# A hybrid encoder step: norms that write into the sum, second projections that turn their own rows, and a residual that is fetched back

## The reference, cut to what matters

```
p = x @ w_in                                   # layer 0: 2560 columns, layer 1: 2888
layer 0: window attention with sinks  |  RWKV-7 time mixing
layer 1: differential attention (C)   |  attention to selected keys (D), picked by an indexer
mix = concat(...) @ w_out
x = layer_norm(ALPHA * x + mix, g1, b1)
h = square(relu(x @ w_up)) @ w_down            # 4096 wide
x = layer_norm(ALPHA * x + h, g2, b2)
```

## Time and profile before

| | |
|---|---|
| timed runs | 4241.22, 4242.47, 4243.46 us; median 4242.47 |
| profiled execution | 4249.11 us, its span 4247.2 us |
| busy share of the span | PE 84%, PEld 76%, DVE 49%, ACT 21%, POOL 4% |
| mean granted TensorE clock | 0.892 of 2.4 GHz |
| DMA | 142.17 MB, mean 33 GB/s |

### The profile page before, as it was taken

How to read it: one execution, slowest core, us unless ns; L and a number is a source line. 1 busy time by engine, 2 the same in 40 slices (tenths; PEclk the granted TensorE clock), 3 DMA queues, 4 the chain that set the end, 5 groups by cost and what they waited for, 6 DMA issues and landing times. The chain is left out here.

```text
span 4247.2 us, 61115 instructions
## 1 busy us (share of the span) xinstructions
PE 3561.4 (84%) x26473; PEld 3233.1 (76%) x26492; DVE 2089.8 (49%) x2992; ACT 909.3 (21%) x1681; POOL 174.7 (4%) x75
## 2 busy tenths in 40 slices
PE   7978499767999999989967777777556889999997
PEld 7977289666999999979954444554434889999996
DVE  4315966556223232441136788998565542323235
ACT  1016311112101001120024444443223120101011
POOL 0010000003000000100020000000000120000001
PEclk9988599878999999989966788887677999999998
DMA  3110000110111111111120000001111111111111
GB/s 100 41 62 5 0 5 4 47 40 25 40 45 45 46 40 45 35 40 43 37 72 1 1 1 1 1 1 30 40 40 25 35 32 44 45 46 45 43 43 47
DMA packets 244534, 142.17 MB, mean 33 GB/s; under 512 B 36101, under 2 KB 237978, under 8 KB 243770
## 3 DMA queue, kind: packets, MB, share of 16 engines
q1 hardware_dynamic: 243320, 138.22, 11.2%
q10 hardware_dynamic: 962, 0.20, 0.0%
HBM read 123.14 MB, written 15.32 MB: 33 GB/s over the span
## 5 line engine op out<-in xcount | busy, mean ns | idle before, releaser
L238 PE MATMUL psum<-rounded,rounded 128*128 128x364 f32 x13536 | 2283.6, 331 | 96.0 <-DVE rounded L744 42.9
L238 PEld LDWEIGHTS psum<-rounded,rounded 128*128 128x128 f32 x13536 | 2273.8, 189 | 107.0 <-issue 81.6
L617 ACT ACTIVATE arena<-psum 128x1092 f32<-128x1092 f32 x64 | 69.3, 1083 | 1216.0 <-PE psum L238 1216.0
L222 DVE CAST rounded<-arena 128x1024 fp32r<-128x1024 f32 x188 | 134.1, 713 | 358.0 <-PE psum L238 343.6
L631 DVE CAST rounded<-arena 128x1092 fp32r<-128x1092 f32 x64 | 46.7, 729 | 535.2 <-ACT arena L620 535.2
L224 DVE TENSOR_TENSOR rounded<-arena,rounded 128x1024 fp32r<-128x1024 f32 x188 | 282.2, 1501 | 6.5
L1388 PE MATMUL psum<-arena 64*64 64x64 f32 x8160 | 256.8, 220 | 23.9 <-POOL arena L1572 12.5
L2063 PE MATMUL psum<-arena 128*128 128x128 f32 (+2 forms) x1424 | 240.1, 323 | 40.5 <-ACT arena L2127 39.5
L1388 PEld LDWEIGHTS psum<-arena 64*64 64x64 f32 x8160 | 246.2, 136 | 35.4 <-DVE arena L1525 18.4
L2063 PEld LDWEIGHTS psum<-arena 128*128 128x128 f32 (+1 forms) x1424 | 215.9, 231 | 66.8 <-issue 37.5
L2047 PE MATMUL psum<-arena 128*128 128x128 f32 (+1 forms) x712 | 142.0, 336 | 139.8 <-ACT arena L2118 139.5
(11 more groups left out here) (230 smaller groups left out, 2762.9 us busy)
## 6 DMA issues: line engine op xcount, KB each, us to landing
arena<-in_w_ff_up SPq DMA_DIRECT2D x128, 256.0 KB, 3.1
arena<-in_w_ff_down SPq DMA_DIRECT2D x128, 256.0 KB, 3.1
arena<-in_w_in_odd SPq DMA_DIRECT2D x46, 256.0 KB, 3.3
arena<-in_w_in_even SPq DMA_DIRECT2D x40, 256.0 KB, 3.4
x_kept<-arena SPq DMA_DIRECT2D x1, 4368.0 KB, 12.4
arena<-x_kept SPq DMA_DIRECT2D x1, 4368.0 KB, 13.1
arena<-in_x_prompt SPq DMA_DIRECT2D x1, 4096.0 KB, 18.4
arena<-in_cache_c_k SPq DMA_DIRECT2D x4, 1024.0 KB, 5.6
```

The costliest lines, as they stand in the source:

```text
L222: nc.vector.tensor_copy(rounded(m, high), low).then_inc(self.weights_high, 1)
L238: last = nc.tensor.matmul(m.ps[:, out:out + TB], rounded(m, w)[:, k, :], rounded(m, x(k))[:, b * TB:(b + 1) * TB], start=(k == 0 and n == ...
```

## The change

The change was described as "mixing inside first projections, norms straight to the sum, second projections with turned rows; residual back later". The diff holds the following.

- `Norm`: no copy of the mean (L716 goes); the centre steps read it from PSUM; five of them stand ahead of the variance, one behind it, two behind the early weight split. Gain and shift are written to a destination `norm.dest`: `m.acc` in the MLPs, `p[:, 8:16]` in the second projections, `m.x` in the last norm. The low part still goes to `m.x`.
- `mlp`: GpSimd's additions and the wait for them go.
- `project_odd` is written out, 23 tiles in a new order: indexer keys and weights (72 columns, one tile), c keys, d keys, c values, d values, then the queries. Tile u - 2 is turned on TensorE inside tile u, at its operand tiles k = 1, 4 and 7, into PSUM banks 3 and 7; VectorE moves the rows of tile u - 3 after the weight split of tile u; SyncE stores key rows from two staging buffers, and all values at the end. The indexer keys are copied to the other 64 partitions by a DMA. The normalised x is written to DRAM (`x_kept`) once all high parts are made. The lambda is made here.
- `turn_rows` goes. `odd_attention` fetches x back at the start of its second block; it has other room for its buffers, and `m.p` has 18 tiles, not 24.
- `Ring` counts its loads per slot (23 is no multiple of 4).

`project_even` is not in the diff.

```diff
 class Norm:
-        act.wait_ge(self.P.sem, self.P.done(0, "mean"))
-        nc.scalar.activation(blocks(self.mean), linear_out(m, 0), ACT.Copy).then_inc(*self.A.step("copy"))
...
-            nc.scalar.activation(m.x[:, k, :], m.x[:, k, :], ACT.Identity, scale=m.col(self.gain + k),
+            nc.scalar.activation(self.dest[:, k, :], m.x[:, k, :], ACT.Identity, scale=m.col(self.gain + k),
...
-                nc.scalar.activation(rounded(m, high[:, k, :]), m.x[:, k, :], ACT.Copy).then_inc(ring.x_high, 1)
+                nc.scalar.activation(rounded(m, high[:, k, :]), self.dest[:, k, :], ACT.Copy).then_inc(ring.x_high, 1)
...
-            tt(m.x[:, k, :], self.source[:, k, :], self.mean, ALU.subtract)\
+            tt(blocks(m.x[:, k, :]), blocks(self.source[:, k, :]), linear_out(m, 0), ALU.subtract)\
...
-            tt(rounded(m, m.x[:, k, :]), m.x[:, k, :], rounded(m, high[:, k, :]), ALU.subtract)\
+            tt(rounded(m, m.x[:, k, :]), self.dest[:, k, :], rounded(m, high[:, k, :]), ALU.subtract)\
...
-        for k in range(3):
+        for k in range(5):
             centre(k)
...
-        centre(3)
+        centre(5)
...
-        for k in range(4, 8):
+        for k in range(6, 8):
             centre(k)
 def mlp(m, layer, norm):
+    norm.dest = m.acc
...
-            for k in range(8):
-                pool.wait_ge(ring.x_split, ring.operands + k + 1)
-                nc.gpsimd.tensor_tensor(m.acc[:, k, :], rounded(m, m.x[:, k, :]), rounded(m, high[:, k, :]), ALU.add)\
-                    .then_inc(residual, 1)
...
-                    dve.wait_ge(residual, layer * 8 + u + 1)
+ODD_TILES = ([("idx", 2816, 17)] + [("ck", 512 + 128 * a, 4 + a) for a in range(4)] + [("dk", 2048, 16)]
+             + [("cv", 1024 + 128 * a, 8 + a) for a in range(4)] + [("dv", 2176, 12)]
+             + [("cq", 128 * a, a) for a in range(4)] + [("iq", 2304 + 128 * a, 12 + a) for a in range(4)]
+             + [("dq", 64 * a, 8 + a) for a in range(4)])
 def project_odd(m, norm):
+    norm.dest = p[:, 8:16, :]
+    groups = [(0, 4), (4, 8), (8, 9)]
+    staged = [p[:, 14 + i, 0:512].rearrange("p (t c) -> p t c", t=4) for i in range(2)]
...
+            for u in range(tiles):                                   # SyncE
+                ring.load(sp, 0, u, True, lambda slot: loads(u, slot))
+                if u == 3:
+                    sp.wait_ge(ring.x_high, ring.operands + 8)
+                    sp.dma_start(io["x_kept"], p[:, 8:16, :].rearrange("p k t -> p (k t)")).then_inc(kept, 16)
+                v = u - 6
+                if v in keys:
+                    store_rows(v)
+                if v == keys[0]:
+                    sp.wait_ge(turned, group_at(v, 2) + 1)
+                    sp.dma_start(p[64:128, 17, :], p[0:64, 17, :]).then_inc(doubled, 16)
+                if v == ODD_TURNED[-1]:
+                    sp.wait_ge(rows, group_at(v, 2) + 1)
+                    store_values("c_v", m.vn)
+                    store_values("d_v", m.vd)
...
+            def turn(u, g):                                          # TensorE
+                n = group_at(u, g)
+                if n >= 2:
+                    pe.wait_ge(rows, n - 1)
+                pe.wait_ge(ring.freed, ring.tiles + u + 1)
+                for t in range(a, z):
+                    last = nc.tensor.transpose(...)
+                last.then_inc(turned, 1)
...
+                def ready(k):
+                    if u == 0:
+                        pe.wait_ge(ring.x_split, ring.operands + k + 1)
+                    if u - 2 in ODD_TURNED and k in (1, 4, 7):
+                        turn(u - 2, k // 3)
...
+            def move(u, g):                                          # VectorE
+                dve.wait_ge(turned, n + 1)
...
+                    to = stores_before(u, g)
+                    if to >= 2:
+                        dve.wait_ge(stored[to % 2], 16 * (to // 2))
...
+            for u in range(1, tiles):
+                ring.split(dve, 0, 0, u, True)
+                if u == 2:
...
+                    dve.wait_ge(kept, 16)
+                if u - 3 in ODD_TURNED:
+                    for g in range(len(groups)):
+                        move(u - 3, g)
-def turn_rows(m):
...
 def odd_attention(m):
+            sp.dma_start(m.arena[:, m.x_at:m.x_at + 8 * T], io["x_kept"]).then_inc(x_back, 16)
...
+            sp.wait_ge(x_back, 16)
             sp.wait_ge(f.O[1].sem, f.O[1].rounds(last_c.round + 4))
```

More of the change, by code:

```diff
@@ L199, in begin @@
         self.ndma = ndma
-        self.next = (self.pieces + pieces, self.loads + pieces // SLOTS * ndma * 16,
+        self.next = (self.pieces + pieces,
+                     [n + len(range(s, pieces, SLOTS)) * ndma * 16 for s, n in enumerate(self.loads)],
                      self.operands + 8, self.tiles + tiles)
@@ L217, in split @@
         low, high = self.low[:, u % SLOTS], self.high[:, u % HIGHS]
-        dve.wait_ge(self.loaded[u % SLOTS], fills * 16 * self.ndma + (self.loads + (u // SLOTS + 1) * 16 * self.ndma))
+        dve.wait_ge(self.loaded[u % SLOTS], fills * 16 * self.ndma + (self.loads[u % SLOTS] + (u // SLOTS + 1) * 16 * self.ndma))
         if not first or u >= HIGHS:
@@ L553, in mlp @@
     ring = m.linears.begin(w + 32 * T, 2, 64, 0)
-    relu, added, squared, hidden_rounded, hidden_split, residual = m.mlp_sems
+    relu, added, squared, hidden_rounded, hidden_split = m.mlp_sems
     had = layer * FF // 128
@@ L692, in tensor @@
         for b in range(NB):
-            last = nc.tensor.matmul(m.ps[:, b * 512:b * 512 + TB], m.c("mean"), m.sum[:, b * TB:(b + 1) * TB],
+            last = nc.tensor.matmul(m.ps[:, b * 512:b * 512 + TB], m.c("mean"), self.totals[0][:, b * TB:(b + 1) * TB],
                                     start=True, stop=True)
         last.then_inc(*self.P.step("mean"))
-        for v, total in enumerate((m.sum, m.square_sum)):
+        for v, total in enumerate(self.totals):
             for t, (b, o) in enumerate(self.spots):
@@ L1971, in queries @@
         t.penal = kind == "D" and t.nk > TOPK
-        t.qtile = 0 if kind == "C" else 12
+        t.qtile = 0 if kind == "C" else 8
         t.load = t.sample and kind == "C"
@@ L2009, in scores @@
         dist = (distS if t.sample else distP)[:, first:first + t.nk]
-        keys = kt_s if t.sample else flat(p[:, ds(i + 4, 1), :]) if t.kind == "C" else p[:, 20, :]
+        keys = kt_s if t.sample else flat(p[:, ds(i + 4, 1), :]) if t.kind == "C" else p[:, 16, :]
         def out(h, b, n):
@@ L2218, in turn_cache_scalar @@
         else:
-            new_k, new_v = p[:, 21 if kind == "I" else 20, TP:TE], m.vd[0:TS, 8, :]
+            new_k, new_v = p[:, 17 if kind == "I" else 16, TP:TE], m.vd[0:TS, 8, :]
         if kind != "I":
@@ L2226, in index_tensor @@
         pe.wait_ge(index_q, t.number + 1)
-        keys, queries_i = (kt_s, qi_s) if t.sample else (p[:, 21, :], qi)
+        keys, queries_i = (kt_s, qi_s) if t.sample else (p[:, 17, :], qi)
         for c, (s, b, n) in enumerate(t.pieces):
@@ L2573, in build @@
     m.mlp_sems = [nc.alloc_semaphore(f"mlp_{n}")
-                  for n in ("relu", "added", "squared", "hidden_high", "hidden_split", "residual")]
+                  for n in ("relu", "added", "squared", "hidden_high", "hidden_split")]
     room(-at[0] % 8)
@@ L2599, in build @@
     norm = Norm(m, "ln1", ROWS["ffng"], ROWS["ffnb"], m.acc)
[L2601 to L2603 removed]
+    m.p = m.arena[:, after_x:after_x + 18 * T].rearrange("p (k t) -> p k t", k=18)
+    m.work = after_x + 18 * T + (9 * 640 + 72)
+    m.ring = m.odd_work = m.work
     assert m.ring + RING <= columns - 8 * T
     project_odd(m, norm)
[L2606 removed]
     odd_attention(m)
@@ L2609, in build @@
     m.ring = m.work
-    project_out(m, "out1", io["w_out_odd"][0], lambda k: m.p[:, k if k < 4 else 8 + k, :], 4)
+    project_out(m, "out1", io["w_out_odd"][0], lambda k: m.p[:, k if k < 4 else 4 + k, :], 4)
     m.work = after_x
```

274 lines of the change are left out of this document (137 added, 137 removed).

## The result

The changed kernel takes 4174.59 us (median of four runs, 4170.59 to 4180.76), the kernel before beside it 4242.97 (4241.22 to 4243.94): a ratio of 0.9841, 95% interval 0.9824 to 0.9858, or 68.4 us less. The forecast was 4179 (4162 to 4207), 63.3 us less. The profiled executions stand 68.35 us apart, 4249.11 and 4180.76 (spans 4247.2 and 4179.0), so they can be compared stage by stage. A step is taken between two marks that both kernels have.

A forecast was written before the change was run, and what follows sets the result against it. TensorE bounds the second projections, VectorE the norm stretches, stores `turn_rows`. Gains of 5.0 + 27.6 + 12.0 + 32.7 less 0.6 and 13.4 make 63.3 us, so 4179 us, range 4162 to 4207.

The forecast's parts named there:

- Residual: MLP starts: without GpSimd's additions, first matmul to second tile's evacuation takes about 30.5 us, 27.6 us less over both.
- Rival 2: MLP norms: GpSimd is not what slows them, so 27.6 us stay; gain 36, time 4207 us; chance 0.05.
- The block `turn_rows`: Between the second projections' last evacuation and the attention's first load: the 33.0 us stretch goes, 32.7 us less.
- One tile, transposes, lambda: Second projections: one tile fewer saves 12.0 us, 99 transposes cost 13.4, lambda's steps 0.6; +2.0 us.
- The upper end of 37 us: Transposes in the second projections: most they could cost, 22 us at clock 0.50 plus 15 for late waits.
- Rival 1: Second projections: late staging or dearer transposes hold the stream, 37 us for 13.4; gain 40, time 4203; chance 0.12.
- The staging loop: Turning tiles: key rows' stores, VectorE's moves and the next turn follow in time, cover 2 us; waits cost nothing.
- The copy to DRAM and back: x_kept's 12.4 us store under the second tile and its load under the attention cost nothing; uncovered some 12 us each.
- Norm fronts: Four norms, mean to first scaling: 1.0, 2.4, 1.0 and 0.6 us less, together 5.0; ends 0 and 9.8.
- The first projections: Stage before the first norm: its mixing steps stand there already and the diff leaves it alone, so no change.
- Rival 3: Turning tiles: the clock falls to 1.2 GHz, 11.98 us more per tile; all eleven, 69 us slower, 4311; chance 0.04.
- Rival 4: Attention: a shifted start moves it either way by some 10 us, 4169 to 4189; chance 0.77 together with the forecast.

The follow-up runs named there:

- e1: The changed kernel with GpSimd's sixteen additions of the two MLPs, and VectorE's waits for them, put back: 4198.93 us.
- e2: The kernel before with the new norm front alone (mean read from PSUM, five parts centred ahead of the variance): 4236.32 us.
- e7: e1 with each GpSimd addition replaced by a one-operand copy of acc onto itself, same places and waits: 4175.60 us.
- e9: e7 with GpSimd's copies held back until VectorE's next scaling is done, so that they start with subtractions: 4181.70 us.
- e3: The changed kernel with each of the 99 transposes into rows done twice: 4185.43 us.
- e6: The changed kernel with nine row buffers for two in the last stage and lambda's products behind the second weight split: 4166.60 us.
- e5: The changed kernel with the rounded x stored three times, both engines waiting for all three, and fetched back four times: 4185.79 us.

## Why the prediction was right, step by step

**Residual.** 27.6 us forecast, 27.6 found, and e1 gives 28.7 when only this is undone. Most of the 1.1 between them comes with the new front: e2, which has it beside the additions, takes 44.87 and 44.69 us where the kernel before takes 44.51 and 44.13. The reason given was a shade off: GpSimd does not make VectorE's operation slower, it makes it wait its turn (e1, e7, e9). The comparison with a norm without GpSimd gave the right size without knowing that, since it measured the whole stretch. Rival 2 is out.

**The block `turn_rows`.** 32.7 forecast, 32.72 found; nothing else came late in its place.

**One tile, transposes, lambda.** +2.0 us forecast, -0.31 found. The term that was mis-sized is the transpose: 0.135 us from the first 24 of `turn_rows`, 0.11 in the stream; 99 of them, some of them narrower, are 10.4 us (e3), not 13.4. The tile is 12.00 us and lambda 0.51 for 0.6 (e6). That makes -1.1. Of the other 0.8 us, some 0.7 are in the tiles without regard to their transposes: plain ones end 12.00 us apart where the kernel before has 11.97, and 21 tiles follow. Why is not known. The evacuations of the kernel before:

```profile
2134.81 1.08 ACT L513 ACTIVATE arena<-psum 128x1092 f32 x1 [10.88 <-PE psum L238]
2146.78 1.08 ACT L513 ACTIVATE arena<-psum 128x1092 f32 x1 [10.89 <-PE psum L238]
```

The upper end of 37 us was held for waits; there were none, and twice or eight times as many transposes add only their own length. The 0.46 us that this end takes for a late wait is marked "issue" in the earlier trace rows, which names no wait. Rival 1 is out.

**The staging loop.** The count put VectorE's third move at 3.7 us after the tile's end, the split's end at 5.7 and the next turn at 6. They came at 4.6, 6.7 and 6.2 (1893.76, 1895.91 and 1895.40 after 1889.18). The order held, but the cover of the turn, from the move's end (1894.04) to its start (1895.40), is 1.4 us, not 2.

**The copy to DRAM and back.** Nothing, as forecast. e5 measures the cover: its third store has landed when VectorE goes on at 1882.14, 11.9 us late, so the place is wanted at about 1870.2. One store is issued at 1847.38 in the changed kernel and lands 13.8 us later (12.4 in the forecast), at 1861.2: 9.0 us before that, and 2.4 before VectorE's next split starts at 1863.58, where the forecast had about 3. Three more fetches lie under the attention.

**Norm fronts.** 5.0 forecast, 8.60 found. At the same clock the forecast's terms hold nearly to the tenth: 1.08, 2.36, 1.16 and 0.50 (second and fourth from e7 and e9), 5.1. The other 3.5 us are the faster sums in two norms of this execution. They were not forecast, and the fronts alone would not have brought them (e7 and e9 lack them); see e2 for what goes with them.

**The first projections** were named as untouched; up to the first norm the two executions differ by 0.4 us.

**The sum.** The pair is 68.3 us apart for 63.3 forecast. Of the 5.0 us, 3.6 are the norm fronts, nearly all of it the clock, and 2.3 the second projections. The stages that were put at nothing move by -0.4, -1.2, +1.5 and +1.1. Executions with the same code there differ by as much: the first norm starts at 1004.27 us in the kernel before and at 1001.37 in e2, and the rest of the first MLP takes 753.6 and 752.6. So the terms were right, and that the total came within 5 us is in part luck. The medians lie 68.4 us apart as well, but a median cannot be taken apart by stage.

**Clock.** Rival 3 (the slower side) needed five tiles at 0.50; there was none, nor at eight times the transposes. Rival 4 came in about its size: from the last evacuation to the third norm the same code takes from 1182.5 (e3) to 1196.7 us (e9), and 1.47 more than before in the pair of the table. Of the 6.6 us between the two profiled executions of the changed kernel the attention makes 6.2 (1196.2 and 1190.0). Single runs of it lie 10 us apart, which fits, but they have no trace.

## What to carry to other kernels

Where two engines slow each other, look at the ends: if the second always ends its own length after the first, they take turns, and the remedy is to move or drop one of the two; VectorE's scaling, which has an operand in PSUM, was not held. The price of moving such work is best read from a stretch of the same kernel that has everything but it. A small operation put into a full TensorE stream cost its own length and no more here; that could be forecast because everything it waits for had been followed to its end with a time beside it. And before a few microseconds of a stage are put down to an edit, compare the same instructions' durations in that stage: here 3.5 us were clock.

## What the runs showed of the hardware

- GpSimd passes and VectorE operations with no operand in the PSUM exclude each other for a whole instruction, whichever comes first: 2.65 us for 1.29 (VectorE second), 2.02 for 1.10 (GpSimd second), and 3.01 for 0.69 for a cast with one operand. VectorE's scaling with one operand from PSUM kept 1.28 us beside either.
- A transpose of a 128 by 128 fp32 piece between matmuls costs 0.11 us at full clock, and tiles with 7.9 of 19.9 us of transposes stayed at 1.00.
- The 36 one-column matmuls of the sums ran at a granted clock of 0.50 or 0.85 in the same place of the same code (7.67 or 4.68 us, 0.85 being a mean over both levels). In eleven traces it went with the moment at which the clock fell in the wait ahead of them: slow at 0.6 to 1.8 us ahead of the mean's first matmul, fast at 2.7 to 3.4 or 0.2 to 0.4. What sets that moment was not found.
